# Second block's feed-forward input: rows normed before the matmuls from the ninth weight slab on

## The reference, cut to what matters

```
h2 = modulate(rmsnorm(x, norm2[l]), sh2, sc2)          # h * (1 + sc2) + sh2
gate, up = jnp.split(h2 @ w_ffn_in[l], 2, axis=-1)     # 1024 -> 2 x 2816
x = x + g2 * ((jax.nn.silu(gate) * up) @ w_ffn_out[l])
```

## Time and profile before

| | us |
|---|---|
| median of three runs | 1425.88 |
| profiled execution, its time | 1428.8 |
| its span, first to last instruction | 1426.1 |
| TensorE busy | 1401.7 (98%) |
| VectorE busy | 1147.6 (80%) |
| ScalarE busy | 822.8 (58%) |
| feed-forward input, first layer of the second block | 834.56 to 962.71 |
| feed-forward input, second layer | 1225.55 to 1353.7 |

### The profile page before, as it was taken

The page is one execution under the profiler, slowest core; times in us unless marked ns, Lnnn a source line. Parts: engine busy times, 40 slices in busy tenths (PEclk is TensorE's granted clock), DMA queues, the critical chain, the costliest instruction groups (busy, mean ns, idle before and its releaser), DMA issues.

```text
span 1426.1 us, 25528 instructions
## 1 busy us (share of the span) xinstructions
PE 1401.7 (98%) x10325; PEld 1312.9 (92%) x10325; DVE 1147.6 (80%) x1805; ACT 822.8 (58%) x1245; POOL 10.5 (1%) x21
## 2 busy tenths in 40 slices
PE   8999999999999999999999999999999999999997
PEld 8898888888888888889999999998999999999986
DVE  7898888888898888887778777777787887777763
ACT  6776776445776775344656555444446575644552
POOL 2000000000000000000000000000000000000000
PEclk9999999999999999999999999999999999999998
DMA  9544999986446999988754578898787556778661
GB/s 263 157 143 117 285 265 272 292 226 163 134 140 191 272 263 297 278 245 225 213 148 148 176 235 224 220 252 227 231 230 217 147 151 184 228 208 235 179 186 65
DMA packets 485363, 297.12 MB, mean 208 GB/s; under 512 B 14956, under 2 KB 455792, under 8 KB 485120
## 3 DMA queue, kind: packets, MB, share of 16 engines
q1 hardware_dynamic: 483728, 292.00, 72.9%
q10 hardware_dynamic: 816, 1.84, 0.4%
q0 software_dynamic: 704, 1.66, 0.3%
HBM read 289.43 MB, written 1.05 MB: 204 GB/s over the span
## 4 chain that ended last, share of the span: by engine, by line
PE 78%; DVE 13%; issue 3%; ACT 3%; DMA 2%; SPq 1%; DVEq 0%; ACTq 0%
PE acc L1938 15%; PE acc L1939 15%; PE acc L1940 14%; PE acc L1955 8%; PE mx L1955 6%; DVE w_lo L1082 5%; PE acc L1956 4%; PE mx L1956 3%; DVE ada_acc L1172 3%; ACT w_hi L583 1%; PE acc L1970 1%; PE acc L1972 1%; PE acc L1971 1%; DMA raw<-in_w_down 1%; DMA rotb<-projb 1%
## 5 line engine op out<-in xcount | busy, mean ns | idle before, releaser
L1082 DVE TENSOR_TENSOR w_lo<-raw,w_hi 128x1024 fp32r<-128x1024 f32 x450 | 541.6, 1221 | 111.2 <-ACT w_hi L583 109.4
L583 ACT ACTIVATE w_hi<-raw 128x1024 fp32r<-128x1024 f32 x450 | 458.0, 1049 | 135.5 <-DMA raw<-in_w_in 82.5
L1938 PE MATMUL acc<-h,w_hi 128*128 128x258 f32 (+1 forms) x1776 | 509.4, 287 | 7.6 <-DVE h L1109 2.8
L1939 PE MATMUL acc<-h,w_hi 128*128 128x258 f32 (+1 forms) x1776 | 503.8, 284 | 0.0
L1940 PE MATMUL acc<-h,w_lo 128*128 128x258 f32 (+1 forms) x1776 | 498.0, 280 | 0.0
L1938 PEld LDWEIGHTS acc<-h,w_hi 128*128 128x128 f32 x1776 | 334.4, 188 | 15.1 <-issue 4.7
L1940 PEld LDWEIGHTS acc<-h,w_lo 128*128 128x128 f32 x1776 | 338.5, 191 | 0.0
L1939 PEld LDWEIGHTS acc<-h,w_hi 128*128 128x128 f32 x1776 | 335.3, 189 | 2.6 <-issue 2.4
L1955 PE MATMUL mx<-u,w_hi 128*128 128x512 f32 x864 | 302.2, 392 | 0.0
L1956 PE MATMUL mx<-u,w_lo 128*128 128x256 f32 x864 | 243.6, 282 | 0.0
L1955 PEld LDWEIGHTS mx<-u,w_hi 128*128 128x128 f32 x864 | 162.2, 188 | 33.2
(11 more groups left out here) (294 smaller groups left out, 1642.8 us busy)
## 6 DMA issues: line engine op xcount, KB each, us to landing
raw<-in_w_in SPq DMA_DIRECT2D x132, 512.0 KB, 4.1
ada<-in_w_ada SPq DMA_DIRECT2D x96, 512.0 KB, 5.1
raw<-in_w_ffn_in SPq DMA_DIRECT2D x88, 512.0 KB, 4.6
raw<-in_w_up SPq DMA_DIRECT2D x64, 512.0 KB, 5.9
raw<-in_w_down SPq DMA_DIRECT2D x64, 512.0 KB, 6.5
raw<-in_w_out SPq DMA_DIRECT2D x32, 512.0 KB, 4.1
raw<-in_w_ffn_out SPq DMA_DIRECT2D x32, 512.0 KB, 4.2
raw<-in_w_ret_o SPq DMA_DIRECT2D x16, 512.0 KB, 4.1
```

The lines of the kernel that those rows point to most:

```text
L583: nc.scalar.activation(w_hi[:, n % NS], raw[:, n % NS], ACT.Copy).then_inc(hi_ready, 1)
L1082: V.tensor_tensor(w_lo[:, n % NS], raw[:, n % NS], w_hi[:, n % NS].bitcast(F32), ALU.subtract).then_inc(lo_ready, 1)
L1938: mm(outp, w_hi[:, i % NS, k], rhs[:, k, 0], start=k == 0, stop=False)
L1939: mm(outp, w_hi[:, i % NS, k], rhs[:, k, 1], start=False, stop=False)
```

## The change

From the ninth slab of the stage on (`FOLD = 8`), TensorE reads new rows `h3`: `xT` times `rstd`, times norm weight and (1 + scale), plus shift, in high and low parts, 256 columns. The first eight slabs are as before. To make `h3`, VectorE multiplies two tiles at a time by `rstd` into `sqt` (`scaled_pair`, four times), ScalarE applies scale and shift twice to each tile, once in float32 into `f_whole` and once rounded into `h3` (`normed_high`, 16 activations), and VectorE subtracts for the low part (`normed_low`, four times). The first two `scaled_pair` stand ahead of round 0, the other steps in rounds 0 to 2. Slab 8 waits, at tiles 0, 2, 4 and 6, for the four low parts in turn.

From round 4 on, VectorE no longer multiplies gate and up by `rstd`: ScalarE takes silu straight from PSUM, and VectorE multiplies the up bank by it straight from PSUM. The PSUM banks are then freed by silu (even slabs) and by the product (odd slabs). The semaphores of `rsqrt_seed` become one that is counted up.

```diff
+FOLD = 8
...
-            sb("under_gt", [P, 22 * 2 * S], F32, ffn)
+            sb("under_h3", [P, 22 * 2 * S], F32, ffn)
+            h3 = sb("h3", [P, KT, 2, S], F32R, ffn)
             gt = sb("gt", [P, 2, W], F32, ffn)
             upv = sb("upv", [P, 2, W], F32, ffn)
+            f_whole = sb("f_whole", [P, 2, 2, S], F32, ffn)
...
+        hn_x = sem("hn_x"); hn_hi = sem("hn_hi"); hn_lo = sem("hn_lo")
+        h_norm = (hn_x, hn_hi, hn_lo)
...
+            logs = [0]
+
+            def rsqrt_seed(r, x, done):
 
                 nc.scalar.activation(r, x, ACT.Ln).then_inc(ln_done, 1)
-                act.wait_ge(ln_done, n + 1)
+                logs[0] += 1
+                act.wait_ge(ln_done, logs[0])
                 nc.scalar.activation(r, r, ACT.Exp, scale=-0.5).then_inc(done, 1)
...
+            def normed_high(counts, n, k, whole, tile, gain, shift):
+
+                ready, high, low = counts
+                b = k // 2
+                act.wait_ge(ready, 4 * n + b + 1)
+                if b >= 2:
+                    act.wait_ge(low, 4 * n + b - 1)
+                nc.scalar.activation(whole[b % 2][:, k % 2], sqt[:, b % 2, k % 2], ACT.Identity, scale=gain(k), bias=shift(k))
+                nc.scalar.activation(tile[:, k, 0], sqt[:, b % 2, k % 2], ACT.Identity, scale=gain(k), bias=shift(k)).then_inc(high, 1)
...
+                def whole_tiles(*tiles):
+                    for k in tiles:
+                        normed_high(h_norm, l, k, (f_whole[:, 0], f_whole[:, 1]), h3, nx2_of(l), lambda k: mod_of(l, 3 * KT + k))
+
                 for u in range(22):
                     at = f0 + 2 * u
                     hi_upto(at + AHEAD)
-                    act.wait_ge(g_scaled, l * 22 + u + 1)
-                    nc.scalar.activation(gt[:, u % 2, 0:S], gt[:, u % 2, 0:S], ACT.Silu, bias=gt[:, u % 2, S:W - 1]).then_inc(g_silu, 1)
+                    if u < FOLD // 2:
+                        act.wait_ge(g_scaled, l * FOLD // 2 + u + 1)
+                        nc.scalar.activation(gt[:, u % 2, 0:S], gt[:, u % 2, 0:S], ACT.Silu, bias=gt[:, u % 2, S:W - 1]).then_inc(g_silu, 1)
+                    else:
+                        act.wait_ge(slab_used, at + 1)
+                        nc.scalar.activation(gt[:, u % 2, 0:S], acc[:, 2 * u % 4, 0:S], ACT.Silu).then_inc(g_silu, 1)
+                    if u < 3:
+                        whole_tiles(3 * u, 3 * u + 1)
                     hi_upto(at + AHEAD + 2)
+                    if u < 2:
+                        whole_tiles(3 * u + 2)
                     act.wait_ge(g_prod, l * 22 + u + 1)
                     nc.scalar.activation(u_hi[:, u], upv[:, u % 2, 0:S], ACT.Copy).then_inc(g_hi, 1)
...
+            def scaled_pair(counts, n, b):
+
+                ready, high, _ = counts
+                if b >= 2:
+                    dve.wait_ge(high, 8 * n + 2 * b - 2)
+                V.tensor_tensor(sqt[:, b % 2], xT[:, 2 * b:2 * b + 2], rstd[:, 0:S].unsqueeze(1).to_broadcast([P, 2, S]),
+                                ALU.mult).then_inc(ready, 1)
+
+            def normed_low(counts, n, b, whole, tile):
+
+                _, high, low = counts
+                dve.wait_ge(high, 8 * n + 2 * b + 2)
+                V.tensor_tensor(tile[:, 2 * b:2 * b + 2, 1], whole[b % 2], tile[:, 2 * b:2 * b + 2, 0].bitcast(F32),
+                                ALU.subtract).then_inc(low, 1)
...
+                scaled_pair(h_norm, l, 0)
+                scaled_pair(h_norm, l, 1)
+
+                def whole_low(b):
+                    normed_low(h_norm, l, b, (f_whole[:, 0], f_whole[:, 1]), h3)
+
                 ada_beside = beside(("F", l))
                 for u in range(22):
                     gate, up = gt[:, u % 2], upv[:, u % 2]
                     sg, su = 2 * u, 2 * u + 1
                     at = f0 + 2 * u
-                    dve.wait_ge(slab_used, at + 1)
-                    V.tensor_tensor(gate, acc[:, sg % 4, 0:W], rstd[:], ALU.mult).then_inc(g_scaled, 1)
+                    if u < FOLD // 2:
+                        dve.wait_ge(slab_used, at + 1)
+                        V.tensor_tensor(gate, acc[:, sg % 4, 0:W], rstd[:], ALU.mult).then_inc(g_scaled, 1)
                     lo_upto(at + AHEAD)
-                    dve.wait_ge(slab_used, at + 2)
-                    V.tensor_tensor(up, acc[:, su % 4, 0:W], rstd[:], ALU.mult).then_inc(g_up, 1)
+                    if u == 1:
+                        whole_low(1)
+                        scaled_pair(h_norm, l, 3)
+                    if u < FOLD // 2:
+                        dve.wait_ge(slab_used, at + 2)
+                        V.tensor_tensor(up, acc[:, su % 4, 0:W], rstd[:], ALU.mult).then_inc(g_up, 1)
                     lo_upto(at + AHEAD + 1)
-                    dve.wait_ge(g_up, l * 22 + u + 1)
                     dve.wait_ge(g_silu, l * 22 + u + 1)
-                    V.scalar_tensor_tensor(up[:, 0:S], up[:, 0:S], up[:, S:S + 1], gate[:, 0:S], ALU.add, ALU.mult).then_inc(g_prod, 1)
+                    if u < FOLD // 2:
+                        dve.wait_ge(g_up, l * FOLD // 2 + u + 1)
+                        V.scalar_tensor_tensor(up[:, 0:S], up[:, 0:S], up[:, S:S + 1], gate[:, 0:S], ALU.add, ALU.mult).then_inc(g_prod, 1)
+                    else:
+                        dve.wait_ge(slab_used, at + 2)
+                        V.tensor_tensor(up[:, 0:S], acc[:, su % 4, 0:S], gate[:, 0:S], ALU.mult).then_inc(g_prod, 1)
+                    if u == 0:
+                        whole_low(0)
+                        scaled_pair(h_norm, l, 2)
+                    if u == 1:
+                        whole_low(2)
+                    if u == 2:
+                        whole_low(3)
                     ada_beside(2 * u)
...
-                    if s >= 4:
-                        pe.wait_ge(g_up if s % 2 else g_scaled, l * 22 + s // 2 - 1)
+                    if s < 4:
+                        pe.wait_ge(x_ready, 8 * (l * 2 + 5) + s + 5)
+                    elif s - 4 < FOLD:
+                        pe.wait_ge(g_up if s % 2 else g_scaled, l * FOLD // 2 + s // 2 - 1)
                     else:
-                        pe.wait_ge(x_ready, 8 * (l * 2 + 5) + s + 5)
+                        pe.wait_ge(g_prod if s % 2 else g_silu, l * 22 + s // 2 - 1)
+                    if s >= FOLD:
+                        slab(f0 + s, h3, acc[:, s % 4, 0:S],
+                             before=(lambda t: pe.wait_ge(hn_lo, l * 4 + t // 2 + 1)) if s == FOLD else None).then_inc(slab_used, 1)
+                        ada_after(s)
+                        continue
```

More of the change, by code:

```diff
@@ L354, in program @@
         n_hi = sem("n_hi"); n_sq = sem("n_sq"); n_acc = sem("n_acc"); h_ready = sem("h_ready")
-        n_ss = sem("n_ss"); n_var = sem("n_var"); n_ln = sem("n_ln"); n_rs = sem("n_rs")
+        n_ss = sem("n_ss"); n_var = sem("n_var"); n_rs = sem("n_rs")
         nx_ready = sem("nx_ready")
@@ L365, in program @@
         g_hi = sem("g_hi"); g_ready = sem("g_ready")
+        hn_x = sem("hn_x"); hn_hi = sem("hn_hi"); hn_lo = sem("hn_lo")
+        h_norm = (hn_x, hn_hi, hn_lo)
         m_ready = sem("m_ready")
         v_t = sem("v_t"); v_sb = sem("v_sb")
-        qk_sq = sem("qk_sq"); qk_ss = sem("qk_ss"); qk_r = sem("qk_r"); qk_ln = sem("qk_ln"); qk_s = sem("qk_s")
+        qk_sq = sem("qk_sq"); qk_ss = sem("qk_ss"); qk_r = sem("qk_r"); qk_s = sem("qk_s")
         qk_e = sem("qk_e"); qk_n = sem("qk_n"); qk_rot = [sem(f"qk_rot{n}") for n in range(2)]; qk_sin = sem("qk_sin"); qk_rope = sem("qk_rope")
@@ L374, in program @@
         f_bc = sem("f_bc"); f_bcsb = sem("f_bcsb"); f_uc = sem("f_uc"); f_ucsb = sem("f_ucsb")
-        f_exp = sem("f_exp"); ml_v = sem("ml_v"); ml_ln = sem("ml_ln"); ml_rs = sem("ml_rs")
+        f_exp = sem("f_exp"); ml_v = sem("ml_v"); ml_rs = sem("ml_rs")
         ml_s = sem("ml_s"); ml_arg = sem("ml_arg"); ml_w = sem("ml_w"); ml_p = sem("ml_p"); ml_nd = sem("ml_nd")
@@ L380, in program @@
         at_t = sem("at_t"); at_pt = sem("at_pt"); at_o = sem("at_o"); at_y = sem("at_y"); at_hi = sem("at_hi")
-        b_ln = sem("b_ln"); b_rs = sem("b_rs")
+        ln_done = sem("ln_done"); b_rs = sem("b_rs")
         b_rot = [sem(f"b_rot{n}") for n in range(2)]; b_sin = sem("b_sin"); b_rope = sem("b_rope"); b_vt = sem("b_vt"); b_vsb = sem("b_vsb")
@@ L584, in hi_upto @@
                     made[0] += 1
-            def rsqrt_seed(r, x, ln_done, done, n):
+            logs = [0]
+            def rsqrt_seed(r, x, done):
                 nc.scalar.activation(r, x, ACT.Ln).then_inc(ln_done, 1)
-                act.wait_ge(ln_done, n + 1)
+                logs[0] += 1
+                act.wait_ge(ln_done, logs[0])
                 nc.scalar.activation(r, r, ACT.Exp, scale=-0.5).then_inc(done, 1)
@@ L616, in norm_seed @@
                 act.wait_ge(n_var, v + 1)
-                rsqrt_seed(rstd[:, 0:width], var[:, 0:width], n_ln, n_rs, v)
+                rsqrt_seed(rstd[:, 0:width], var[:, 0:width], n_rs)
```

(8 more changed lines are left out.)

## The result

The changed kernel takes 1434.59 us (median of four runs, 1434.06 to 1437.3), the kernel before 1425.99 (four runs, 1425.37 to 1426.44): a ratio of 1.0065, 95% interval 1.0049 to 1.0082. It is slower, by 8.6 us in 1426. The forecast was 1436.5 with 1431.5 to 1440.5 around it.

A forecast was written before the change was run, and what follows sets the result against it. TensorE, busy 98%, was taken to bound the kernel. Per layer 1.21 + 0.63 + 3.59 - 1.64 = 3.79, with the clock 5.31; both layers 10.6 us over the median 1425.88 gave 1436.5, range 1431.5 to 1440.5.

The forecast's parts named there:

- What bounds: Whole kernel: TensorE, busy 98% at full clock; VectorE or ScalarE time in the steady stage is worth nothing.
- Slab 3, +1.21 us: Start of slab 3: two scaled pairs ahead of the gate multiply delay w_lo(3), so TensorE starts 1.21 us later.
- Slab 8's bank, +0.63 us: Start of slab 8: TensorE waits for gate 2's bank, starting at 860.23 instead of 859.60, +0.63 us.
- The walk: Rounds 0 to 3: operation times stepped through in the diff's order with measured spacings, giving each late start.
- The hole, +3.59 us: Slab 8 before its seventh tile: TensorE stands from 862.36 to 865.95 for the last normed_low, +3.59 us.
- The bound taken for the Identities: ScalarE's 16 Identity activations: spaced 0.49 us apart; the lower bound was 0.40.
- The clock, +1.52 us a layer: Behind slab 8's hole: granted clock 0.50 for 3.4 us, costing 1.52 us a layer, bounds 0 and 1.52.
- no fall, or in one layer only: Rival: holes come, but the clock does not fall, or in one layer only: 1433.5, 1435.0; chance 0.20.
- The narrow matmuls, -1.64 us a layer: From slab 8 on, 36 slabs a layer: 256 columns instead of 258 save 0.045 us each, 1.64 us a layer.
- SyncE and the freed banks, no cost: SyncE's later ada load has 7 us of cover; banks freed by silu and product are wanted 8.5 us later: no cost.
- The sum: Both layers: 1.21 + 0.63 + 3.59 - 1.64 = 3.79 a layer, 5.31 with the clock, 10.6 us together.

The follow-up runs named there:

- e2: Kernel before plus two unread 128x512 multiplies by rstd on VectorE ahead of round 0: 1427.51 us against 1424.79, ratio 1.0018.
- e5: The changed kernel again, unedited, on another chip than the e1, e2 and e4 runs: 1432.70 us against 1425.64, ratio 1.0053.
- e12: The changed kernel, unaltered, five runs beside e11 on one chip: 1434.49 us against 1425.57, ratio 1.0062.
- e11: Changed kernel with 27 matmuls into an unread bank where TensorE would stand in slab 8: 1431.13 us against 1425.57, ratio 1.0042.
- the filled one: Changed kernel with 27 matmuls into an unread bank before tile 6 of slab 8: 1432.14 us, ratio 1.0054; repeated as e11, 1431.13 us.
- e1: Kernel before, slabs 8 to 43 reading only 256 columns of the old h2 rows, without shift: 1425.08 us against 1424.79, ratio 1.0000.
- e7: e4 with the rows of h3 258 words apart, still 256 columns: ratio to the kernel before 0.9983 to 1.0002.
- e6: Kernel before with rows of h2 264 words apart instead of 258, still 258 columns: slabs 2.89 us against 2.87, not quicker.
- e10: e4 with the rows of h3 264 words apart, 256 columns: slabs at 2.83 us.
- e4: Changed kernel with FOLD = 12 and the pairs, low parts and Identities spread over later places: 1420.62 us against 1424.79, ratio 0.9972.
- e8: Changed kernel with FOLD = 12 alone, same work in the same places: 1429.30 us against 1425.64, ratio 1.0034.
- e9: Kernel before with rows of h2 272 words apart, still 258 columns: slab rate kept within 0.01 us, not quicker.

## Why the prediction was right, step by step

- **What bounds.** Right. VectorE lost 13.9 us of work and ScalarE gained 15.8, and neither shows in the time but where TensorE waits. In the second layer the pieces are the same to 0.02 us up to slab 8.
- **Slab 3, +1.21 us.** Right to 0.01 us, in each of the changed kernel's profiles and alone in e2. The new multiplies take 689 ns (686 forecast), spaced by 0.61.
- **Slab 8's bank, +0.63 us.** Measured +0.55 and +0.57. The walk had gate 2 at 859.67; the stage began 0.90 us earlier in this execution (833.66 for 834.56), and gate 2 stands at 858.78, which is 859.68 on the walk's scale.
- **The hole, +3.59 us.** The waiting was 3.58 - 0.12 = 3.46 and 3.52. What the late starts cost at slab 8 is a little more, since the first step behind a wait is longer than 0.12 us too: without a fall of the clock slab 8 takes 6.53 us (e5, second layer) where its like take 2.80, so 3.73. The walk had the last `normed_low` at 865.12; it began at 864.24, that is 865.14. Rows of the timelines of VectorE and then of ScalarE in the changed kernel, to be followed with the walk:

```profile
858.78 0.42 DVE L1927 TENSOR_TENSOR gt<-acc,rstd 128x258 f32<-128x258 f32 x1
...
862.70 1.23 DVE L1113 TENSOR_TENSOR w_lo<-raw,w_hi 128x1024 fp32r<-128x1024 f32 x1 [3.17 <-ACT w_hi L589]
863.84 0.48 DVE L1939 SCALAR_TENSOR_TENSOR upv<-upv,gt 128x256 f32<-128x256 f32 x1
864.24 0.69 DVE L1237 TENSOR_TENSOR h<-f_whole,h 128x512 fp32r<-128x512 f32 x1
```

ScalarE:

```profile
859.23 0.51 ACT L1076 ACTIVATE gt<-gt 128x256 f32<-128x256 f32 x1 [2.26 <-DVE gt L1927]
859.65 0.59 ACT L635 ACTIVATE f_whole<-sqt,modT,nx 128x256 f32<-128x256 f32 x1
860.14 0.59 ACT L636 ACTIVATE h<-sqt,modT,nx 128x256 fp32r<-128x256 f32 x1
...
861.63 1.99 ACT L589 ACTIVATE w_hi<-raw 128x1024 fp32r<-128x1024 f32 x2
```

  Gate 2 releases silu 2; four Identities (ScalarE's activations that apply scale and shift), 0.49 us apart, stand between it and the rounding of `w_hi(10)`; VectorE waits 3.17 us for that with the product and the last low part queued behind it. The bound taken for the Identities (0.49, not 0.40) is what made the step come out.
- **The clock, +1.52 us a layer.** Right in this profile: pieces 8 and 9 cost 5.02 and 5.18 against 3.58 without a fall, so 1.44 and 1.60. But it is not a constant. Over the three profiled executions of the changed kernel six equal holes were followed by no fall (once), 3.4 us (three times) and 6.8 us (twice), at 0, 1.44 to 1.60, and 2.45 to 2.58 us. The 3.4 us for both layers in e12 against e11 are what such cases gave over five runs of each. That the execution profiled here had just one fall of 3.4 us in each layer, as forecast, is in part luck: neither of the other two had. The prediction gave the case "no fall, or in one layer only" 0.20; e5 is one of those, in one layer.
- **The narrow matmuls, -1.64 us a layer.** The step of which the size and the reason were wrong. The size: slabs 10 to 43 gave 2.47 us in most layers of the changed kernel and of the filled one (34 x 0.073; slabs at 2.80), but 2.18 and 1.28 in the execution that is profiled here, where some of the slabs ran at 2.83 and 2.88; over 34 slabs the forecast has 1.64 x 34 / 36 = 1.55. A wider look at the kernel before would have shown the quicker rate too. Its `y2` slabs ran at two rates; the prediction took the stretch of the earlier trace rows, and this one, TensorE alone, has 190 matmuls in 22.17 us by their starts, 116.7 ns each:

```profile
778.30:800.50 22.20, 22.20 (x193) 1.00 0.58 179
```

  The reason: the prediction compared 256 columns in rows 256 apart with 258 in rows 258 apart and gave the difference to the columns. e1 and e7 show that the columns without the close rows are worth 0.1 to 0.8 ns a matmul. That the wrong reason did no harm is luck: the change happens to make both at once. The Trainium skill (TensorE: Matmul & The Clock Gate, section "Wait — 56ns, not 53.3ns?") gives about 0.8 ns for two columns; e1's two stages, 0.8 and 0.1, lie at that and below it, whereas 258 to 256 columns at a distance of 264 (e6 to e10) is 2.5 ns (2.89 and 2.83 us over 24). The step from start to start that this section gives for 256 columns, by estimate 109.2 ns, is met nowhere: the shortest here is 116.7.
- **SyncE and the freed banks, no cost.** Right. The fourth `ada` load is issued at 870.97, near 871.9 on the walk's scale (872 forecast), and from slab 9 on TensorE waits for nothing up to the end of the stage. Silu from PSUM takes 384 ns and the product 424, less than the forms before, not more.

The sum was 10.6 us for both layers and the two stages gave 10.3: up to slab 9, with the holes and the clock, 13.7 as walked, and slabs 10 to 43 gave back 3.5 where 3.1 stood. So close a match is in part luck, for the stages of the other two profiled executions of the changed kernel gave 8.3 (e5) and 9.7 (e12). The rest of the miss is not the kernel's: this execution came to the first of the stages 0.9 us earlier, and what lies between span and time is 1.8 us and not 2.7. The median, 1.9 us under the forecast, lies lower than the profiled execution by 2.7; what the single clock falls cost in its other runs no profile shows.

What I did not see was that both holes can be avoided, for the price of four narrow slabs a layer. The rows had it: ScalarE waits 43.7 us and VectorE 23.8 us in a stage, and it was the order, not the sum of the work, that made them late; e4 shows it with 12 to 13 us.

## What to carry to other kernels

Side work on an engine with slack still costs its full length where that engine happens to be late: put new work behind the operation that the bottleneck is waiting for, spread it over the rounds in which the engine waits, and start using its result some rounds later (two in e4). A hole of the bottleneck must be priced with the lowered clock that may follow it (here 0 to 2.6 us on top of 3.5), and as a range. Before a rate is carried over from another stage, compare everything in which the two operands differ, the distance of their rows too.

## What the hardware did that I had not expected

- **The same matmul has several rates at a full clock.** In the profiled execution of the changed kernel, one layer ran at 120.0 ns a matmul over 336 matmuls (14 slabs in 40.32 us) and then at 116.7 over 312 (13 slabs in 36.40 us; a window also counts matmuls that reach over its edges), with the same operands and the same granted clock:

```profile
1265.67:1305.99 40.32, 40.32 (x338) 40.32 (x337) 28.87 (x39) 21.66 (x32) 0.00 (x0) 1.00 0.78 226
1312.12:1348.52 36.40, 36.40 (x314) 36.40 (x313) 25.99 (x36) 17.21 (x25) 0.00 (x0) 1.00 0.68 199
```

  The rate changed behind a few matmuls of another job in between (the transposes of the `ada` results), and in e5, e11 and e12 the same stretch ran at 116.7. The gain of 1.28 instead of 2.47 us in the second layer comes from this. It is not alone: slabs went from 2.83 to 2.80 us in the first layer of this execution and of e8, and from 2.87 to 2.85 in e1 and e7, each time behind such a break. So a rate read in one stretch can be that of the stretch and not of the form. Its cause is open.
- **The distance of the moving operand's rows changes the rate**, by up to 0.07 us a slab of 2.8 from 256 to 258 words (e4 and e7), with no simple order in the rest of the table above.
- **Equal holes, unequal clocks.** Six holes of 3.3 us of idle time gave 0, 3.4 or 6.8 us at 1.2 GHz, and one of 1.90 us (e8) gave none. The two falls of 6.8 us began 1.1 and 1.4 us before TensorE resumed (e5, first layer; e12, second). The hole near 667 us, which the clock term was made from the earlier trace rows, is not the same in each execution: from start to start it was 2.13 us in the kernel before, 2.60 in the changed one and 2.40 in e9, each followed by 3.4 us at half clock, and 2.63 us in e2, 1.99 in e1 and 1.87 in e12, followed by none. So neither the length of a hole nor the program tells whether the clock will fall, in the range from 2.0 to 3.6 us from start to start; what else decides is open.
